# Three passes of 96 places per expert, in place of two of 128, in a two-block transformer kernel

## What is computed

```python
def moe_swiglu(x, w_router, b_router, w1, w3, w2):
    logits = (x @ w_router).astype(jnp.float32) + b_router.astype(jnp.float32)
    top_vals, top_idx = lax.top_k(logits, TOP_K)
    top_w = jax.nn.softmax(top_vals, axis=-1)
    gates = jnp.sum(jax.nn.one_hot(top_idx, N_EXPERTS, dtype=jnp.float32) * top_w[..., None], axis=-2)
    out = jnp.zeros_like(x)
    for e in range(N_EXPERTS):
        out = out + gates[..., e:e + 1].astype(x.dtype) * _swiglu(x, w1[e], w3[e], w2[e])
    return out
```

## Time and profile before

| | |
|---|---|
| median of 3 runs | 2018.97 us (2016.92 to 2020.2) |
| span of the profiled execution | 2018.5 us |
| mean granted TensorE clock | 0.996 of full |
| TensorE busy | 98% of the span |
| VectorE, ScalarE, GpSimd busy | 79%, 50%, 3% |
| experts, first product to last | 712.7 to about 1668 us |

### The profile page before, as it was taken

One profiled execution on the slowest core, in us unless ns is written; L12 is line 12 of the kernel. 1 busy time (PEld: TensorE's weight loads), 2 busy tenths in 40 slices (PEclk: granted clock), 3 DMA queues, 4 the chain that ended last, 5 costly groups with the idle time before them and its releaser, 6 DMA issues.

```text
span 2018.5 us, 27225 instructions
## 1 busy us (share of the span) xinstructions
PE 1982.4 (98%) x10728; PEld 1676.7 (83%) x10728; DVE 1603.9 (79%) x1618; ACT 1017.1 (50%) x1047; POOL 59.0 (3%) x53
## 2 busy tenths in 40 slices
PE   8999999999999999999999999999999998999999
PEld 7988788889988778888888888888888887868887
DVE  3676688886666698888888888888888975668987
ACT  0264110021453377777777777777777753472000
POOL 0110100000000200000000000000000000100000
PEclk9999999999999899999999999999999999999999
DMA  9643588753634589999999999999999985445650
GB/s 322 195 164 110 181 296 315 271 165 122 211 124 178 222 298 384 380 380 370 384 384 377 384 380 379 373 385 384 382 384 371 408 287 164 135 126 167 205 175 37
DMA packets 184217, 553.15 MB, mean 274 GB/s; under 512 B 9296, under 2 KB 112080, under 8 KB 140864
## 3 DMA queue, kind: packets, MB, share of 16 engines
q1 hardware_dynamic: 175296, 517.55, 69.7%
q10 hardware_dynamic: 6912, 25.02, 3.2%
q0 software_dynamic: 1920, 9.34, 1.2%
HBM read 528.02 MB, written 23.59 MB: 273 GB/s over the span
## 4 chain that ended last, share of the span: by engine, by line
PE 93%; DVE 3%; ACT 3%; issue 1%; DMA 0%; DVEq 0%; ACTq 0%; SPq 0%
PE act_ps L1190 30%; PE dve_ps L1215 15%; PE act_ps L1040 9%; PE job_ps L1144 6%; PE act_ps L1112 4%; PE dve_ps L1112 4%; PE dve_ps L916 4%; PE dve_ps L1040 2%; PE act_ps L1087 2%; PE job_ps L1067 2%; PE act_ps L1111 2%; PE dve_ps L1111 2%; PE act_ps L916 1%; PE job_ps L1198 1%; PE job_ps L967 1%
## 5 line engine op out<-in xcount | busy, mean ns | idle before, releaser
L2482 DVE TENSOR_TENSOR weights_rest<-weight_ring,expert_short 128x2048 fp32r<-128x2048 f32 x336 | 762.9, 2289 | 103.2 <-ACT expert_short L1781 102.6
L1781 ACT ACTIVATE expert_short<-weight_ring 128x2048 fp32r<-128x2048 f32 x336 | 641.0, 1916 | 109.9 <-PE act_ps L1190 74.1
L1190 PE MATMUL act_ps<-expert_short,tokens_short 128*128 128x512 f32 x896 | 354.2, 395 | 3.9 <-ACT arena_o L1798 2.0
L1190 PE MATMUL act_ps<-expert_short,tokens_rest 128*128 128x512 f32 x896 | 349.2, 390 | 0.0
L1190 PE MATMUL act_ps<-weights_rest,tokens_short 128*128 128x512 f32 x896 | 349.1, 390 | 0.0
L1190 PEld LDWEIGHTS act_ps<-expert_short,tokens_short 128*128 128x128 f32 x896 | 168.2, 188 | 38.7 <-DVE weights_rest L2482 3.2
L1190 PEld LDWEIGHTS act_ps<-expert_short,tokens_rest 128*128 128x128 f32 x896 | 168.2, 188 | 36.3
L1190 PEld LDWEIGHTS act_ps<-weights_rest,tokens_short 128*128 128x128 f32 x896 | 168.4, 188 | 33.6
L1767 ACT ACTIVATE arena_mla<-arena_mla 128x512 f32<-128x512 f32 x22 | 14.0, 634 | 298.4 <-DVE arena_mla L2415 298.4
L2402 DVE TENSOR_TENSOR weights_rest<-weight_ring,ffn_weights_short 128x2048 fp32r<-128x2048 f32 x66 | 151.3, 2292 | 2.2
L1215 PE MATMUL dve_ps<-expert_short,hidden_short 128*128 128x512 f32 x440 | 137.1, 393 | 0.0
(11 more groups left out here) (421 smaller groups left out, 3518.3 us busy)
## 6 DMA issues: line engine op xcount, KB each, us to landing
weight_ring<-in_moe_w SPq DMA_DIRECT2D x336, 1024.0 KB, 6.8
weight_ring<-in_w_in SPq DMA_DIRECT2D x43, 1024.0 KB, 8.0
weight_ring<-in_ffn_w SPq DMA_DIRECT2D x32, 1024.0 KB, 7.8
weight_ring<-in_w_out SPq DMA_DIRECT2D x12, 1024.0 KB, 6.8
weight_ring<-in_w_gate SPq DMA_DIRECT2D x11, 1024.0 KB, 5.3
weight_ring<-in_w_up SPq DMA_DIRECT2D x11, 1024.0 KB, 8.1
weight_ring<-in_w_down SPq DMA_DIRECT2D x10, 1024.0 KB, 7.0
weight_ring<-in_w_ple_gate SPq DMA_DIRECT2D x8, 1024.0 KB, 6.2
```

Of the source, the lines that this page charges most:

```text
L1190: m = nc.tensor.matmul(bank[0:CAP, :], a[:, 4 * c + k, :], w[:, k, :], start=(c == k == i == 0), stop=(c == 1 and k == 3 and i == 2))
L1781: nc.scalar.activation(shorts[u % SHORTS][:, :], ring[:, slot, half], ACT.Copy).then_inc(moe_w_short, 1)
L2482: V.tensor_tensor(ring_lo[slot][:, half], ring[:, slot, half], shorts[u % SHORTS][:, :], ALU.subtract)\
```

## The change

`CAP` becomes 96, and `PASSES` follows as 3. Where the code took `CAP` and 128 for the same number, the two are told apart: the identity of the transposes is cut to 96 x 96, the group of 512 hidden columns keeps its width under a name of its own, and the cleared groups stay 128 rows high, now 18 instead of 16 for each buffer. The gates of a middle pass need two conditions.

```diff
-CAP = P
+CAP = 96
 PASSES = -(-SEQ // CAP)
+CLEARED = EXPERTS * PASSES * CAP // P
+assert CLEARED * P == EXPERTS * PASSES * CAP
...
-        small = sb("small", [P, 96])
+        small = sb("small", [P, 96 + 4 * PASSES])
...
-        GROUP_W = 4 * CAP
+        GROUP_W, FF_GROUP = 4 * CAP, 4 * P
...
-        moe_h = arena_o[:, 0:GROUP_W]
+        moe_h = arena_o[:, 0:FF_GROUP]
...
-        ROWS_CLEAR = 16 * (2 * EXPERTS * PASSES - 1)
+        ROWS_CLEAR = 16 * (2 * CLEARED - 1)
...
-        turn_gates = [small[:, 86 + 4 * i:90 + 4 * i] for i in range(PASSES)]
+        turn_gates = [small[:, 96 + 4 * i:100 + 4 * i] for i in range(PASSES)]
...
                         m = nc.tensor.transpose(job_ps[k // 4][:, (k % 4) * CAP:(k % 4 + 1) * CAP],
-                                                rows[0:CAP, k * P:(k + 1) * P], const("ident"))
+                                                rows[0:CAP, k * P:(k + 1) * P], const("ident")[0:CAP, 0:CAP])
...
                         m = nc.tensor.transpose(job_ps[2 + g % 2][:, j * CAP:(j + 1) * CAP], moe_h[0:CAP, j * P:(j + 1) * P],
-                                                const("ident"))
+                                                const("ident")[0:CAP, 0:CAP])
...
-                            m = nc.tensor.transpose(job_ps[0][0:CAP, i * P:(i + 1) * P], pick_gate[:, i, :], const("ident"))
+                            m = nc.tensor.transpose(job_ps[0][0:CAP, i * P:(i + 1) * P], pick_gate[:, i, 0:CAP], const("ident"))
...
-                    for f in (2 * pair, 2 * pair + 1) if clear and 2 * pair < EXPERTS * PASSES else ():
-                        group = slice(f * CAP, (f + 1) * CAP)
+                    for f in (2 * pair, 2 * pair + 1) if clear and 2 * pair < CLEARED else ():
+                        group = slice(f * P, (f + 1) * P)
...
-                act.dma_start(x_rows[:, :], rows_in.rearrange("(n r) d -> n r d", r=CAP)[PASSES * e + turn]).then_inc(x_rows_here, 16)
+                act.dma_start(x_rows[0:CAP, :], rows_in.rearrange("(n r) d -> n r d", r=CAP)[PASSES * e + turn]).then_inc(x_rows_here, 16)
...
-                    nc.scalar.activation(moe_h[0:CAP, :], act_ps[0][0:CAP, 0:GROUP_W], ACT.Silu).then_inc(moe_silu_done, 1)
+                    nc.scalar.activation(moe_h[0:CAP, :], act_ps[0][0:CAP, 0:FF_GROUP], ACT.Silu).then_inc(moe_silu_done, 1)
...
                     V.scalar_tensor_tensor(turn_gates[0], rank, float(CAP), kept, ALU.is_lt, ALU.mult)
-                    V.scalar_tensor_tensor(turn_gates[1], rank, float(CAP), kept, ALU.is_ge, ALU.mult)
+                    for later in range(1, PASSES):
+                        m = V.scalar_tensor_tensor(turn_gates[later], rank, float(later * CAP), kept, ALU.is_ge, ALU.mult)
+                    step(m)
+                    for later in range(1, PASSES - 1):
+                        V.scalar_tensor_tensor(turn_gates[later], rank, float((later + 1) * CAP), turn_gates[later], ALU.is_lt, ALU.mult)
                     step(V.scalar_tensor_tensor(by_k(row_f), expert_of, EXPERTS - 1.0, gate, ALU.is_equal, ALU.mult))
```

More of the change, by code:

```diff
@@ L2497, in hidden @@
                     dve.wait_ge(moe_unit_done, it * UNITS + (moe_unit_of("w3", g, 1) + 1))
-                    V.tensor_tensor(moe_h[0:CAP, :], act_ps[1][0:CAP, 0:GROUP_W], moe_h[0:CAP, :], ALU.mult)\
+                    V.tensor_tensor(moe_h[0:CAP, :], act_ps[1][0:CAP, 0:FF_GROUP], moe_h[0:CAP, :], ALU.mult)\
                         .then_inc(moe_h_full, 1)
@@ L2509, in last_rows @@
                         for i in range(QT):
-                            m = V.tensor_scalar(pick_gate[:, i, :], const("iota"), last_place[:, i:i + 1], last_gate[:, i:i + 1],
+                            m = V.tensor_scalar(pick_gate[:, i, 0:CAP], const("iota"), last_place[:, i:i + 1], last_gate[:, i:i + 1],
                                                 ALU.is_equal, ALU.mult)
```

## The result

The changed kernel takes 2027.39 us, the median of 4 runs (2027.02 to 2029.92), against 2019.10 us for the kernel before in 4 runs (2016.92 to 2020.20). The ratio is 1.0044, with an interval of 1.0032 to 1.0056. It is slower, by 8.3 us, and outside the predicted range.

A forecast was written before the change was run, and what follows sets the result against it. The prediction took TensorE alone, product after product, as the bound. Savings of 13.6 us (products), 7.7 (transposes) and 0.4 (copies), 21.7 us in all, from the median 2018.97 gave 1997.3 us; range 1987 to 2017 us.

The forecast's parts named there:

- The bound: Through a whole expert the chain is TensorE alone; a nanosecond on each of 4032 products is worth 4.03 us.
- One pass: Experts' token passes: the fullest expert has 92 tokens, under 96, so the other two passes stay out; 336 units.
- Term 1: Expert products: the 13.5 ns beside the columns shrink with load width to 10.1 ns; 13.6 us less.
- Term 2: Experts' 288 float32 transposes: 96 moving columns instead of 128 save 26.6 ns each; 7.7 us less.
- Term 3: Copies of turned values shrink from 512 to 384 elements; on the path once, before the first product; 0.4 us less.
- Term 4: Silu, multiplication, `token_gates`, four more DMAs, row fetches and stores, put-back: together put at nothing.
- Fixed extra: Products' 13.5 ns are a weight switch blind to width; only transposes and copies gain; 2010.9 us, chance 0.21.
- Slower: Products: stationary operands under 128 columns are loaded in the open, 66 ns more each; about 2279 us, chance 0.13.

The follow-up runs named there:

- e3: Kernel before, with products loading only columns 0 to 95 of each tile, transposes left wide; 2027.79 us.
- e5: Kernel before, with products loading only columns 0 to 111 of each tile; 2030.58 us.
- e6: Kernel before, with products loading only columns 0 to 63 and products of the places from 64 on left out; 2028.33 us.
- e7: Kernel before, with products loading only columns 0 to 31 and products of the places from 32 on left out; 2035.84 us.
- e10: Kernel before, loads untouched, with the 512 moving columns starting 32 columns late for three blocks of four; 2035.72 us.
- e11: Kernel before, with load and moving columns both starting 32 columns late, for three tiles and three moving blocks of four; 2025.68 us.
- e12: Kernel before, 128 places and two passes, with only the transposes narrowed to 96 moving columns; 2011.87 us, ratio 0.9968.
- e1: Changed kernel with tiles 128 columns apart again and all 128 columns loaded, transposes still moving 96; 2010.88 us, ratio 0.9963.
- e2: Changed kernel with tiles 128 columns apart again, but only 96 columns loaded; 2021.92 us.
- e9: Kernel before, with 128-column loads starting 32 columns late for the first three tiles of four, moving columns untouched; 2037.47 us.
- e4: Kernel before, with loads still 128 columns wide but starting 96 columns (384 bytes) apart; 2033.84 us.

## Why the prediction was wrong

**The bound** held. The chain is TensorE alone, and a nanosecond per product is worth 4 us. That reading is why so small a change of pace decided the case.

**One pass** held (336 units).

**Term 1 is the step that failed.** I took the 13.5 ns beside the columns to be read time that the load takes from the moving stream, and so to go with the data loaded, 13.5 x 96/128. Its two supports were that they are absent in float32 and at the lower clock. Both hold for anything that matters only when columns pass at the full rate (and "none" in float32 was rounded: 429 - 426 leaves 3 ns, as 227 - 213 leaves 14 in fp32r); they say nothing of how the extra goes with the load's width, and no row had a second width. The width runs e3, e5, e6 and e7 show it: no shrinking at all, and a step of about 3 ns upwards. In place of 13.6 us less came 16.7 us more; that swing of 30.3 us is the whole of the 30.1 us between forecast and result. My bounds let the term fall by up to 54 us and rise only if a load came into the open. A small rise had no reason in my list, so I gave it no room; but an unknown that no row shows had to be open on both sides.

The Trainium skill, TensorE: Matmul & The Clock Gate, section Step-by-step: what each phase is for, says that loading the next weights takes no read bandwidth from the running matmul. I had not weighed it; by it term 1 is zero. The widths agree with it against me, since less data brought nothing. e10 and e11 go beyond it: the two are not independent, as their relative place changes the pace.

I also overlooked that `CAP` sets the tiles' distance as well as the load's width. The diff shows it in the shapes of `x_hi` and `h_hi`, which stay written with `CAP` and so need no edit. A change of a constant has to be followed into every address that is made from it.

**Term 2** held: 82.5 ns a transpose, 7.7 us, and e12 measures 6.5 us for it alone. A transpose is not held by its load.

**Term 3** held in its durations: L2505 took 551 ns for 550 forecast, and on the path VectorE's two copies took 1.02 us for 1.29. Its 0.4 us of the whole is too small for the runs to show.

```profile
709.19 1.02 DVE L2491 TENSOR_TENSOR tokens_rest<-job_ps,tokens_short 128x384 fp32r<-128x384 f32 x2 [1.76 <-ACT tokens_short L1792]
```

**Term 4** held to within those some 2 us, by e12 against e1.

**The rivals.** *Fixed extra* came nearest: terms 2 and 3 alone and 2010.9 us forecast, near e1_wide's 2010.88, but only once the loads are wide and in place again. That the two numbers are the same is luck: e1_wide has term 2 alone, and its kernel before stood at 2018.42. *Slower* named the right sign and the right threshold: 15.4 ns beside the columns, reckoned from 13.5, is 1.9 ns more, and the change brought 4.1. Its mechanism fell. Loads stay hidden even at 96 columns (e2, e3), and it was priced at 66 ns where 4.1 came. The rule of the Trainium skill, TensorE: Matmul & The Clock Gate, section Weight-path perf modes, that fast weight load is on for 128 weights in a type other than FP32, doesn't show either: a load's record falls from 188 to 161 ns with 96 columns, so no fast load was lost.

**What stays open:** why a load under 128 columns costs some 3 ns when it is in place; why 112 columns have two paces and alternate between them; why in `up` of e9 and e10 products with a like pair are slow too, and in e4 those beside a tile at its old place (229 to 232 ns); and what the base of 13.5 ns is, which no run here removed.

## What to carry to other kernels

When a stationary operand needs fewer than 128 columns, narrow only what moves, here the identity of the transposes, and go on loading full tiles that start as the moving blocks do: e1_wide has the 96 places and gains 0.37%, the change as made loses 0.44%. (Nearly all of that gain is the transposes', by e12.) When a constant is changed, list the addresses and strides that it sets beside the counts. An extra of 13 ns whose cause is unknown is not to be scaled; bound it on both sides of zero, and where TensorE is the whole chain, multiply that by the number of products before choosing a sign.

## What the runs showed of the hardware

- In fp32r, with 512 moving columns, a product is 227.5 ns from the next with a load of 128 columns that starts in step. Loads of 112, 96 and 64 columns make it 230.5 (a mean of two paces, 229 and 233), 230.1 and 230.1, and 32 make it 231.7.
- A load whose start stands 128 bytes off the moving block's place costs 4 to 5 ns on average (e9 232.2, e10 232.0, against 227.5), also when only the moving block was moved. In e11, both moved by 128 bytes cost nothing where they go together (226.5 to 227.8). In `up` of e9 and e10 the few products whose load and moving columns start alike are as slow as the rest.
- The two faults don't add: 96 columns and tiles 384 bytes apart give 231.7, full loads from such tiles 231.6.
- A load's record shortens by 26 to 27 ns for each 32 columns less (188, 161, 135 and 109 at 128, 96, 64 and 32), but none of these narrower loads makes the products come faster than the full one does.
- A float32 transpose with 96 moving columns takes 82.5 ns, with 128 it takes 109.
